# Folding the memory norm's weight into the weight splits, a second queue for the first slab, a finish by halves, and a later head scaling

## The chip, the cores and the metric

The kernel runs on one core of a Trainium2 chip. The metric is device time in microseconds from launch to the end of the program; the median of three runs of the kernel before is 1544.7 us (1544.7 to 1545.28).

## The reference

256 tokens of width 1024 go through two layers. Each layer is a mixer followed by a feed-forward part:

```
h = rms_norm(x, norm_g);  proj = h @ w_in                      # 1024 x 6672
q_a, k_a = rms_norm per head (8 heads of 64)  -> stick-breaking attention
gated linear attention, 4 heads, chunks of 64 -> o_b
mkv = rms_norm(mem, mem_norm_g) @ w_mem_kv                     # mem: 256 x 1024
m_k, m_v = split(mkv);  q_c, k_c = rms_norm per head (4 heads of 128)
o_c = softmax(q_c k_c^T) m_v
x = x + (sum_b sigmoid(gate_b) * (o_b @ w_br_b)) @ w_out
layer 0: x = x + swiglu(rms_norm(x))           # width 2816
layer 1: x = x + mixture of 8 experts, top 2   # width 3584 each
```

`rms_norm(y, g)` is `y * rsqrt(mean(y*y) + 1e-6) * g`. The factor `rsqrt(...)` belongs to a row (a token), the weight `g` to a column of `y`, which is a row of the weight matrix that follows.

## The kernel before

**Trunk.** Everything up to the experts is a list of products (`product_table`): first `mem_k` (the memory times its key weights), then `sb_q`, `sb_k`, `sb_v`, `mem_v` and so on. A product of width 512 takes its weights in four slabs of 128 x 1024 floats (512 KB). SyncE (SP) issues the slab loads in order into five buffers `w_raw`. ScalarE (ACT) rounds each slab to `w_hi` (`split`, L943), VectorE (DVE) forms the rest `w_lo = w_raw - w_hi` (`splits_until`, L1305), four slabs ahead of their use, and TensorE (PE) makes three passes (L2010 to L2012), so that a slab is 12 matmuls of 512 columns. The left operands are split in the same way: PE transposes a token tile into `ps` (`turn_tokens`, L1926), ACT takes the high part (L979), DVE the low part (L1340, `turned`).

**Order around the products.** Each engine's program is written by one function, `in_order`. After a slab, each engine calls `side()`, which runs the next step of a waiting generator, up to a `yield`; so a generator's yields decide behind which slab a step stands. `finish` runs the rest of a generator.

**The start.** SP loads memory tile 0, then `mem_norm_g` broadcast to 128 rows (512 KB), then memory tile 1, then slabs 0 and 1, then `x`, then slabs 2 on. PE passes the time with `idle_turns`. DVE multiplies each memory tile by the weight (L1354), into the buffers `tok` and `sq`, and signals `norm_done`; PE transposes these. Only the row factor `mem_rstd` is applied later, by ACT, when it takes the product out of PSUM. Then `x` is normalised: ACT squares it (L969) only after slabs 0 to 3 have been split (`splits_until(4)` in `x_norm`), DVE and GpSimd (POOL, L776) form the row factor, and DVE normalises (L1327) with `mix_norm_g`, which POOL's own DMA brings into the same `gain` buffer once the memory tiles have been weighted. The transposes of `x` into `xt1` stand behind the third slab of `mem_k` (two yields in `x_turn`), and `sb_q` needs them. POOL writes twenty small loads (`mixer_constants`, L745 to L751, for both layers) and a row of constants before it comes to the first head norm.

**The memory in layer 1.** `mem` is reloaded into `hn`; its mean squares, row factor and normalisation are made anew during the last feed-forward product.

**Head norms.** After `mem_k`, `sb_q`, `sb_k` and `ca_q`, ACT takes the result to `tok` and its squares to `sq`. DVE reduces the squares (L1513), POOL raises to the power -1/2 (L816), and DVE scales `tok` (L1526), in the first `side()` of the next product, that is behind one slab split. Three yields later PE transposes the scaled heads (L2134) and DVE writes them with their weight (L1537).

**Experts.** The experts' 1 MB slabs (`exp_raw`) stream from HBM through 22 buffers. Slots 0 to 6 are written out; later ones run in a loop whose last six slabs come one by one, each with a semaphore (`end_ready`). PE multiplies by four lanes of 32 tokens (L2140, a helper's line). At the very end, ACT copies the output block `ps` to `hs` (L1279), `scatter_last` multiplies by the selection, token tile 0 into `ps` and tile 1 into `pa`; DVE adds each whole tile to `xs` (L1895) and SP stores each tile (L708).

Of the kernel before, what the change touches and what calls it, by code (L numbers as in the profile page):

```python
# [5 lines left out]
F32 = mybir.dt.float32  # L6
# [3 lines left out]
ALU = mybir.AluOpType  # L10
# [24 lines left out]
RAW, SPLIT = 5, 5  # L35
AHEAD = SPLIT - 1
# [55 lines left out]
GAINS = 16 * LAYERS * 10  # L92
# [80 lines left out]
def trunk(nc, x_in, mem_in, mix_norm_g, w_in, sb_q_g, sb_k_g, gla_a_up, gla_a_b, gla_o_g, ca_q_g,  # L173
# [10 lines left out]
    with ExitStack() as ctx:  # L184
# [26 lines left out]
        with ExitStack() as trunk_only:  # L211
# [25 lines left out]
            cum_tri = early("cum_tri", [P, P])  # L237

# [93 lines left out]
        mem_reloaded, first_gain = sem("mem_reloaded"), sem("first_gain")  # L332
# [31 lines left out]
        y_hi, last_y = sem("y_hi"), sem("last_y")  # L364
        stored, tail_scattered = sem("stored"), sem("tail_scattered")
# [3 lines left out]
        end_ready = [sem(f"end_ready{i}") for i in range(EXP_SLABS - END)]  # L369

# [71 lines left out]
        def raw_slot(j):  # L442
            return w_raw[:, j % RAW, :]

# [113 lines left out]

        def turned_half(t, half):
            return ps[:, t * DM:(t + 1) * DM][:, half].rearrange("p (k t) -> p k t", t=P)  # L560
# [34 lines left out]
        def _(sp):  # L595
            sp.dma_start(hn[:, 0, :], memory_in[:, 0, :]).then_inc(first_tile[0], 16)
            sp.dma_start(gain[:, :], mem_norm_g[0].rearrange("(o d) -> o d", o=1)
                         .broadcast_to([P, DM])).then_inc(first_gain, 16)
            sp.dma_start(hn[:, 1, :], memory_in[:, 1, :]).then_inc(first_tile[1], 16)
# [57 lines left out]
            def expert_slabs(e, i):  # L657
# [8 lines left out]
                for j in range(end, EXP_SLABS):  # L666
                    sp.wait_ge(slab_used, i * EXP_SLABS + (PRE + j + 1 - EXP_RAW))
                    sp.dma_start(exp_slots[place(i, j)], moe_slabs[bass.ds(e, 1), j // LOAD, :, j % LOAD, :]
                                 .rearrange("e p n -> (e p) n"))\
                        .then_inc(end_ready[j - END], 16)  # L670

            first = first_slabs()
            for s, src in enumerate(flat):
                if s == 2:
                    sp.dma_start(xs[:, :, :], tokens).then_inc(x_loaded, 16)
                if s == 8 * RAW:
                    sp.dma_start(route_w[:, :, :], moe_router[0].rearrange("(k p) n -> p k n", p=P))\
                        .then_inc(route_loaded, 16)
                    with nc.allow_non_contiguous_dma(reason="1024 numbers, once"):
                        sp.dma_start(route_g[:, :],  # L680
                                     ffn_norm_g[LAYERS - 1].rearrange("(k p) -> p k", p=P))\
                            .then_inc(route_loaded, 16)
                if s >= RAW:
                    sp.wait_ge(lo_ready, s - RAW + 1)
                dst = raw_slot(s)[:, 0:sizes[s]]
                if len(src.shape) == 3:
                    dst = dst.rearrange("p (k n) -> p k n", k=src.shape[1])
                sp.dma_start(dst, src).then_inc(raw_ready[s % RAW], 16)
# [17 lines left out]
            for t in range(NT):  # L706
                sp.wait_ge(added, slots * NT + (t + 1))
                sp.dma_start(result[:, t, :], xs[:, t, :]).then_inc(stored, 16)  # L708
            sp.wait_ge(stored, NT * 16)
# [3 lines left out]
        def _(pool):  # L713
# [8 lines left out]
            gain_order = [g[l] for l in range(LAYERS) for g in (mem_norm_g, mix_norm_g, ffn_norm_g)]  # L722

            def load_gain(k):
                pool.wait_ge(norm_done, NT * k)
# [3 lines left out]
            def start():  # L729
# [6 lines left out]
                load_gain(1)  # L736
                inverse_root(mem_rstd)

            def mixer_constants():
                link(pool.memset(a_up[:, :, :], 0.0))  # L740
                for l in range(LAYERS):
                    for i, (g, n) in enumerate(((sb_q_g, SB_DH), (sb_k_g, SB_DH), (gla_o_g, GLA_DV),
                                                (ca_q_g, CA_DH), (ca_k_g, CA_DH))):
                        for r in range(0, P, n):
                            pool.dma_start(head_gains[r:r + n, l, i:i + 1],  # L745
                                           g[l].rearrange("(d o) -> d o", o=1),
                                           allow_slow_non_contiguous=True).then_inc(gains_loaded, 16)
                    for r in (0, GATE_RANK):
                        pool.dma_start(a_up[r:r + GATE_RANK, l, :], gla_a_up[l])\
# [1810 lines left out]
```

## Time and profile before

| | |
|---|---|
| median of three runs | 1544.7 us |
| profiled execution, its own time | 1545.91 us |
| its span | 1543.2 us |
| PE / DVE / ACT / POOL busy | 1499.5 / 553.9 / 430.9 / 83.5 us |
| HBM read | 477.34 MB |

The span runs from the first to the last instruction; the execution's time is 2.7 us longer. All starts are microseconds from the span's start. A PE matmul's shown duration is longer than its share of the pipeline: matmuls of one kind start closer together than they last.

### The profile page before, as it was taken

What the parts mean: (1) busy time and instruction counts of PE and PEld (TensorE: products, weight loads), DVE (VectorE), ACT (ScalarE), POOL (GpSimd) and SP (SyncE); (2) the same over time, 40 slices, a digit from 0 to 9 for tenths busy, and PEclk for the clock granted to TensorE, in tenths of its full rate; (3) what the DMA queues carried; (4) which work ended last, traced back from release to release, by engine and by line L of the source; (5) the groups of instructions that cost most, each with busy time, mean ns of one, the idle gap of its engine ahead of it and who ended that gap; (6) DMA issues with size and microseconds to landing.
All of it is one profiled execution on the core that took longest, in us unless ns stands there. A gap on an engine that the chain in (4) does not pass through costs nothing.

```text
span 1543.2 us, 27981 instructions
## 1 busy us (share of the span) xinstructions
PE 1499.5 (97%) x12518; PEld 906.8 (59%) x12518; DVE 553.9 (36%) x668; ACT 430.9 (28%) x551; POOL 83.5 (5%) x130
## 2 busy tenths in 40 slices
PE   8999999999999999999999999999999999999778
PEld 6888888788888887888335333353323533533222
DVE  5755576655567655666400101001010110010101
ACT  5556654544445557554000000000000000000000
POOL 5211100000002111001000000000000000000000
PEclk9999999999999999999999999999999999999999
DMA  8555454765655555677999999999999999999996
GB/s 274 178 152 166 149 164 153 231 189 170 205 189 184 174 149 161 207 298 306 418 403 402 416 429 429 428 428 428 428 430 429 427 428 427 430 427 427 433 426 258
DMA packets 86231, 480.20 MB, mean 311 GB/s; under 512 B 11296, under 2 KB 13408, under 8 KB 64096
## 3 DMA queue, kind: packets, MB, share of 16 engines
q1 hardware_dynamic: 84480, 474.67, 79.2%
q0 software_dynamic: 1632, 3.74, 0.8%
q8 instruction: 98, 1.61, 0.4%
q14 instruction: 21, 0.17, 0.0%
HBM read 477.34 MB, written 1.05 MB: 310 GB/s over the span
## 4 chain that ended last, share of the span: by engine, by line
PE 83%; DMA 11%; DVE 2%; POOL 2%; issue 0%; ACT 0%; SPq 0%; DVEq 0%; POOLq 0%
PE pa L2140 26%; PE ps L2140 17%; PE pa L2010 13%; PE pa L2012 12%; PE pa L2011 12%; DMA exp_raw<-in_moe_slabs 11%; DVE w_lo L1305 1%; POOL hrs L816 1%; PE ps L1926 1%; POOL head_gains L745 0%; DMA gain<-in_mem_norm_g 0%; PE ps L2313 0%; PE ps L2134 0%; PE pa L2045 0%; DVE xt L1340 0%
## 5 line engine op out<-in xcount | busy, mean ns | idle before, releaser
L2140 PE MATMUL pa<-exp_raw,xf 128*32 128x512 f32 (+1 forms) x5104 | 489.8, 540 | 20.4 <-DMA exp_raw<-in_moe_slabs 17.8
L2140 PEld LDWEIGHTS pa<-exp_raw,xf 128*32 128x32 f32 x5104 | 162.8, 110 | 327.8 <-issue 268.4
L1305 DVE TENSOR_TENSOR w_lo<-w_raw,w_hi 128x1024 fp32r<-128x1024 f32 x226 | 274.2, 1231 | 122.1 <-ACT w_hi L943 113.0
L943 ACT ACTIVATE w_hi<-w_raw 128x1024 fp32r<-128x1024 f32 (+1 forms) x228 | 236.9, 1053 | 148.7 <-PE pa L2012 147.1
L2140 PE MATMUL ps<-exp_raw,hf 128*32 128x256 f32 (+1 forms) x3040 | 245.3, 413 | 8.5 <-DMA exp_raw<-in_moe_slabs 8.2
L2010 PE MATMUL pa<-w_hi,r 128*128 128x512 f32 x600 | 240.3, 400 | 1.9 <-DVE r L1340 1.8
L2012 PE MATMUL pa<-w_hi,r 128*128 128x512 f32 x600 | 234.6, 391 | 0.0
L2011 PE MATMUL pa<-w_lo,r 128*128 128x512 f32 x600 | 234.6, 391 | 0.0
L1873 DVE TENSOR_TENSOR hs<-pa,hs 128x768 f32<-128x768 f32 (+3 forms) x32 | 23.7, 741 | 584.3 <-ACT hs L1268 584.3
L1268 ACT ACTIVATE hs<-pa 128x768 f32<-128x768 f32 (+3 forms) x32 | 20.4, 637 | 659.5 <-PE pa L2140 659.5
L2140 PEld LDWEIGHTS ps<-exp_raw,hf 128*32 128x32 f32 (+1 forms) x3040 | 116.1, 114 | 137.2 <-issue 68.8
L2010 PEld LDWEIGHTS pa<-w_hi,r 128*128 128x128 f32 x600 | 113.1, 188 | 29.4 <-issue 3.2
L2012 PEld LDWEIGHTS pa<-w_hi,r 128*128 128x128 f32 x600 | 113.0, 188 | 24.4
L2010 PE MATMUL pa<-w_hi,xt 128*128 128x512 f32 (+1 forms) x320 | 123.2, 385 | 3.0 <-DVE xt L1340 2.7
L2011 PEld LDWEIGHTS pa<-w_lo,r 128*128 128x128 f32 x600 | 113.2, 189 | 22.0
L2012 PE MATMUL pa<-w_hi,xt 128*128 128x512 f32 (+1 forms) x320 | 121.3, 379 | 0.0
L2011 PE MATMUL pa<-w_lo,xt 128*128 128x512 f32 (+1 forms) x320 | 121.3, 379 | 0.0
L2010 PEld LDWEIGHTS pa<-w_hi,xt 128*128 128x128 f32 x320 | 60.2, 188 | 16.1 <-issue 2.7
L2012 PEld LDWEIGHTS pa<-w_hi,xt 128*128 128x128 f32 x320 | 60.2, 188 | 11.3
L2011 PEld LDWEIGHTS pa<-w_lo,xt 128*128 128x128 f32 x320 | 60.3, 188 | 10.6
L1858 DVE TENSOR_TENSOR yf<-ps,yf 128x768 fp32r<-128x768 f32 (+1 forms) x7 | 5.9, 844 | 88.7 <-ACT yf L1255 88.7
L1255 ACT ACTIVATE yf<-ps 128x768 fp32r<-128x768 f32 (+1 forms) x7 | 5.0, 719 | 96.8 <-PE ps L2140 96.8
(281 smaller groups left out, 813.2 us busy)
## 6 DMA issues: line engine op xcount, KB each, us to landing
exp_raw<-in_moe_slabs SPq DMA_DIRECT2D x82, 3072.0 KB, 32.3
exp_raw<-in_moe_slabs SPq DMA_DIRECT2D x87, 1024.0 KB, 8.2
w_raw<-in_w_in SPq DMA_DIRECT2D x104, 512.0 KB, 4.4
w_raw<-in_ff_w_gate_up SPq DMA_DIRECT2D x44, 512.0 KB, 4.5
w_raw<-in_ff_w_down SPq DMA_DIRECT2D x22, 512.0 KB, 4.1
w_raw<-in_w_mem_kv SPq DMA_DIRECT2D x16, 512.0 KB, 5.1
w_raw<-in_w_out SPq DMA_DIRECT2D x16, 512.0 KB, 4.3
w_raw<-in_w_br_sb SPq DMA_DIRECT2D x8, 512.0 KB, 3.5
```

The lines of the kernel that those rows point to most:

```text
L816: pool.tensor_tensor(dst[:, 0:n], src[:, 0:n], half[:, 0:n], ALU.pow)\
L943: act.activation(dst, raw, ACT.Copy).then_inc(hi_ready, 1)
L1255: act.activation(yf[:, 0, 0:blocks * OUT], ps[:, 0:blocks * OUT], ACT.Copy)\
L1268: act.activation(hidden_rows(s, blocks), gate_up(s, 0, blocks), ACT.Silu)\
L1305: dve.tensor_tensor(dst, raw, hi.bitcast(F32), ALU.subtract)\
L1858: dve.tensor_tensor(yf[:, 1, 0:blocks * OUT], ps[:, 0:blocks * OUT], yf[:, 0, 0:blocks * OUT].bitcast(F32), ALU.subtract)\
L1873: dve.tensor_tensor(hidden_rows(s, blocks), gate_up(s, 1, blocks), hidden_rows(s, blocks), ALU.mult).then_inc(e_h, 1)
L1926: ins = pe.transpose(banks[:, t * DM + k * P:t * DM + (k + 1) * P], src[:, k * P:(k + 1) * P], ident[:, :])
L2010: pe.matmul(dst, hi, m_hi, start=first, stop=False)
L2011: pe.matmul(dst, hi, m_lo, start=False, stop=False)
L2012: return pe.matmul(dst, lo, m_hi, start=False, stop=last)
L2140: return pe.matmul(dst, a, b, start=start, stop=stop, skip_group_check=True)
```

## The change

Seven edits, in the order of the program:

1. Memory tiles go straight into `start_x` (the buffers `tok` and `sq`), unweighted, and are transposed as they are; the load of broadcast `mem_norm_g` and DVE's two multiplications go. `mem_norm_g` of both layers comes as 16 rows of 128 floats by a DMA on ACT's queue, PE turns it into 16 columns (`mem_gain`), DVE copies these. For the 16 slabs of `mem_k` and `mem_v`, the split multiplies each half slab by its column: two ACTIVATEs with a scale and two `scalar_tensor_tensor` instead of one of each.
2. Slab 0 is loaded from ACT's queue (`FIRST_ACT = 1`); SP begins with slab 1. `x` stands before slab 3. POOL loads `mix_norm_g` once slab 1 has landed.
3. In layer 0 `x` is squared after three slabs are split, not four; it is transposed behind the first slab of `mem_k`; slab 0 is multiplied tile by tile. The memory's row factor is made after that, behind the second slab, and kept for layer 1, where the memory's squares, row factor and normalisation go.
4. POOL's small loads are made per layer, ten at a time; the constants come after the first head norm.
5. DVE's head scaling stands behind the second slab split of the next product.
6. In the expert loop the last slab is loaded in two halves with a semaphore each.
7. At the end ACT copies two halves; `scatter_last` works by halves, token tile 0 into `pa` first and tile 1 into `ps`; DVE adds four half tiles and SP stores four.

Seven idle turns stand at PE's start instead of twelve, and five instead of six before the first product.

```diff
-            sp.dma_start(hn[:, 0, :], memory_in[:, 0, :]).then_inc(first_tile[0], 16)
-            sp.dma_start(gain[:, :], mem_norm_g[0].rearrange("(o d) -> o d", o=1)
-                         .broadcast_to([P, DM])).then_inc(first_gain, 16)
-            sp.dma_start(hn[:, 1, :], memory_in[:, 1, :]).then_inc(first_tile[1], 16)
+            sp.dma_start(start_x[0], memory_in[:, 0, :]).then_inc(first_tile[0], 16)
+            sp.dma_start(start_x[1], memory_in[:, 1, :]).then_inc(first_tile[1], 16)
...
+                    sp.dma_start(dst[:, 0:DM], src[:, 0:DM]).then_inc(end_ready[j - END], 16)
+                    sp.dma_start(dst[:, DM:], src[:, DM:]).then_inc(last_half_ready, 16)
...                       # GpSimd, start()
-                load_gain(1)
-                inverse_root(mem_rstd)
+                pool.wait_ge(raw_ready[1], 16)
+                load_gain(0)
...                       # ScalarE, split(s)
+                for cols, scale in gain_halves(s):
+                    if s == 0:
+                        act.wait_ge(mem_gain_ready, 1)
+                    ins = act.activation(dst[:, cols], raw[:, cols], ACT.Copy, scale=scale)
...                       # ScalarE, start()
+                act.dma_start(mem_rows[:, :], mem_norm_g.rearrange("l (k p) -> (l k) p", p=P))\
+                    .then_inc(mem_rows_loaded, 16)
+                for s in range(FIRST_ACT):
+                    act.dma_start(raw_columns(s), flat[s]).then_inc(raw_ready[s % RAW], 16)
...                       # x_turn on ACT, DVE (and PE without memory_norm)
-                yield
-                yield
+                if l > 0:
+                    yield
+                    yield
                 for t in range(NT):
                     turned(xt1, ps, t)
                 yield
+                if l == 0:
+                    memory_norm()
...                       # VectorE, x_norm
                 if l == 0:
-                    splits_until(4)
+                    splits_until(3)
                     dve.wait_ge(x_loaded, 16)
                 for t in range(NT):
                     mean_square(t)
-                dve.wait_ge(turn_ready, turns)
+                if l > 0:
+                    dve.wait_ge(turn_ready, turns)
                 for t in range(NT):
-                    normalise(xs, t)
+                    normalise(xs, t, l)
+                if l == 0:
+                    splits_until(4)
...                       # VectorE, head_work
-                dve.wait_ge(head_rs, heads)
+                heads_then = heads
+                yield
+                dve.wait_ge(head_rs, heads_then)
...                       # VectorE, the end
-            for t, bank in enumerate((ps, pa)):
+            for t, bank in enumerate((pa, ps)):
                 dve.wait_ge(tail_scattered, t + 1)
-                dve.scalar_tensor_tensor(out=xs[:, t, :], in0=bank[:, 0:DM],
...
+                for half in (LEFT, RIGHT):
+                    dve.scalar_tensor_tensor(out=xs[:, t, half], in0=bank[:, half],
...                       # TensorE, start() and the first product
-                idle_turns(12, 0)
-                for t in range(NT):
-                    turn_tokens(True, ps, t, True)
-                idle_turns(6, 0)
+                idle_turns(7, 0)
+                turn_tokens(False, ps, 0, True)
+                pe.wait_ge(mem_rows_loaded, 16)
+                pe.matmul(gain_columns, mem_rows[:, :], ident[0:LAYERS * KT, 0:LAYERS * KT],
+                          start=True, stop=True).then_inc(mem_rows_turned, 1)
+                turn_tokens(False, ps, 1, True)
+                idle_turns(5, 0)
...
+                        if p is table[0] and g == 0:
+                            for t in range(NT):
+                                pe.wait_ge(turn_lo, t + 1)
+                                ins = multiply(0, [t])
+                            ins.then_inc(slab_used, 1)
+                            side()
+                            continue
...                       # TensorE, down(), in the loop of experts
+                            if kk == 1 and j == EXP_SLABS - 1 and type(i) is not int:
+                                pe.wait_ge(last_half_ready, i * 16 + 16 * (1 - len(BLOCKS_AT)))
```

## Rows read from the trace of the kernel before

**Rows 1.** The page: PE's busy time, and PE, DMA and bandwidth in 40 slices

```profile
PE 1499.5 (97%) x12518; PEld 906.8 (59%) x12518; DVE 553.9 (36%) x668; ACT 430.9 (28%) x551; POOL 83.5 (5%) x130
...
GB/s 274 178 152 166 149 164 153 231 189 170 205 189 184 174 149 161 207 298 306 418 403 402 416 429 429 428 428 428 428 430 429 427 428 427 430 427 427 433 426 258
```

**Rows 2.** Busy time by stretch: length; PE, PEld, DVE, ACT, POOL; granted clock; DMA share, GB/s

```profile
11.60:13.60 2.00, 0.00 (x0) 0.00 (x0) 1.96 (x2) 2.00 (x3) 0.00 (x0) 1.00 1.03 396
...
27.70:29.50 1.80, 0.01 (x1) 0.00 (x0) 1.77 (x2) 1.76 (x4) 1.80 (x4) 1.00 0.84 199
30.00:33.40 3.40, 3.40 (x10) 2.62 (x9) 3.33 (x5) 1.11 (x2) 3.40 (x8) 0.50 0.79 271
...
52.70:64.50 11.80, 11.80 (x58) 9.87 (x57) 8.76 (x12) 6.07 (x8) 3.74 (x1) 1.00 0.55 181
```

**Rows 3.** Timeline of the start: start us, length us, engine, line, instruction, count, idle before

```profile
1.74 4.99 PE L1933 MATMUL pa<-ident 128*128 128x128 f32 x24 [1.74 <-POOL ident L732]
...
9.11 1.09 PE L1926 MATMUL ps<-ident,sq 128*128 128x128 f32 x8
...
12.34 1.22 DVE L1340 TENSOR_TENSOR xt<-ps,xt 128x1024 fp32r<-128x1024 f32 x1
...
13.61 0.50 PE L2010 MATMUL pa<-w_hi,xt 128*128 128x512 f32 x1 [2.07 <-DVE xt L1340]
```

**Rows 4.** DMA issues of the start: KB each, us from issue to landing

```profile
hn<-in_mem SPq DMA_DIRECT2D x1, 512.0 KB, 3.3
...
w_raw<-in_w_mem_kv SPq DMA_DIRECT2D x1, 512.0 KB, 8.3
...
gain<-in_mix_norm_g POOLq DMA_DIRECT2D x1, 512.0 KB, 7.2
...
xs<-in_x SPq DMA_DIRECT2D x1, 1024.0 KB, 10.3
```

**Rows 5.** Timeline: x's load, its squares, row factors and normalisation, then sb_q's start

```profile
3.17 0.57 SPq L675 DMA_DIRECT2D xs<-in_x  x1
...
18.46 1.05 ACT L969 ACTIVATE gates<-xs 128x1024 f32<-128x1024 f32 x1
...
20.79 1.28 DVE L1327 SCALAR_TENSOR_TENSOR hn<-xs,nrstd,gain 128x1024 f32<-128x1024 f32 x1
20.97 1.51 POOL L776 TENSOR_TENSOR nrstd<-nms,half 128x1 f32<-128x1 f32 x1 [0.40 <-DVE nms L1320]
...
29.53 0.50 PE L2010 MATMUL pa<-w_hi,r 128*128 128x512 f32 x1 [1.82 <-DVE r L1340]
```

**Rows 6.** Timeline of one head norm, and the one place where PE waits for one

```profile
47.71 3.75 POOL L816 TENSOR_TENSOR hrs<-hms,half 128x16 f32<-128x16 f32 x1 [8.09 <-DVE hms L1517]
...
51.50 1.29 DVE L1526 TENSOR_TENSOR tok<-tok,hrs 128x512 f32<-128x512 f32 x2 [2.80 <-POOL hrs L816]
...
69.68 0.93 PE L2140 MATMUL ps<-qT,kT 64*128 64x256 f32 x8 [0.22 <-DVEq L1546]
```

**Rows 7.** PE's waits in 100 to 560: for whom, us in total, times, longest

```profile
PE pa L2010 <- DVE xt L1340: 0.7, 1, 0.7
```

**Rows 8.** Timeline of the end

```profile
1523.72 0.39 ACT L1268 ACTIVATE hs<-pa 128x256 f32<-128x256 f32 x1 [16.77 <-PE pa L2140]
...
1533.51 1.94 PE L2140 MATMUL ps<-exp_raw,hf 128*64 128x512 f32 x8 [0.44 <-DMA exp_raw<-in_moe_slabs]
...
1535.50 0.60 ACT L1279 ACTIVATE hs<-ps 128x512 f32<-128x512 f32 x1 [11.39 <-PE ps L2140]
...
1537.52 1.28 DVE L1895 SCALAR_TENSOR_TENSOR xs<-ps,small,xs 128x1024 f32<-128x1024 f32 x1 [11.88 <-PE ps L2140]
1538.72 1.28 DVE L1895 SCALAR_TENSOR_TENSOR xs<-pa,small,xs 128x1024 f32<-128x1024 f32 x1
```

**Rows 9.** The two stores, and the weighting of a half tile by DVE

```profile
out<-xs SPq DMA_DIRECT2D x2, 512.0 KB, 2.7
...
L1401 DVE TENSOR_TENSOR hn<-xs,gain x4: 684/692/693, 274.7 to 282.0; 128x512 f32<-128x512 f32 x4
```

More of the change, by code:

```diff
@@ L35 @@
 RAW, SPLIT = 5, 5
+FIRST_ACT = 1
 AHEAD = SPLIT - 1
@@ L557, in trunk, with gain_halves @@
         start_x = [a[:, :, :].rearrange("p t c -> p (t c)") for a in (tok, sq)]
+        gain_columns = pa[:, 3 * BW:3 * BW + LAYERS * KT]
+        def gain_halves(s):
+            for p in table:
+                if p.name in ("mem_k", "mem_v") and p.first <= s < p.end:
+                    per = SLAB // p.width
+                    k = p.layer * KT + (s - p.first) * per
+                    return [(slice(n * p.width, (n + 1) * p.width), mem_gain[:, k + n:k + n + 1])
+                            for n in range(per)]
+            return []
         def turned_half(t, half):
@@ L705, in _ @@
                 expert_slabs(e, i)
-            for t in range(NT):
-                sp.wait_ge(added, slots * NT + (t + 1))
-                sp.dma_start(result[:, t, :], xs[:, t, :]).then_inc(stored, 16)
-            sp.wait_ge(stored, NT * 16)
+            for n in range(2 * NT):
+                t, half = n // 2, (LEFT, RIGHT)[n % 2]
+                sp.wait_ge(last_added, n + 1)
+                sp.dma_start(result[:, t, half], xs[:, t, half]).then_inc(stored, 16)
+            sp.wait_ge(stored, 2 * NT * 16)
         @block.gpsimd
@@ L720, in link @@
                 pool.wait_ge(pool_step, steps)
-            gain_order = [g[l] for l in range(LAYERS) for g in (mem_norm_g, mix_norm_g, ffn_norm_g)]
+            gain_order = [g[l] for l in range(LAYERS) for g in (mix_norm_g, ffn_norm_g)]
             def load_gain(k):
-                pool.wait_ge(norm_done, NT * k)
+                if k > 0:
+                    pool.wait_ge(norm_done, NT * k)
                 pool.dma_start(gain[:, :], gain_order[k].rearrange("(o d) -> o d", o=1)
@@ L1057, in product @@
                 l = p.layer
-                first_memory = l == 0 and p.name in ("mem_k", "mem_v")
+                of_memory = p.name in ("mem_k", "mem_v")
+                first_memory = l == 0 and of_memory
                 if first_memory:
-                    act.wait_ge(norm_rs, NT)
+                    act.wait_ge(norm_rs, NT * 2)
                 def root(t):
@@ L1278, in _ @@
             act.wait_ge(slab_used, slots * EXP_SLABS + PRE)
-            act.activation(hs[:, 0:FEW_BLOCKS * OUT], ps[:, 0:FEW_BLOCKS * OUT], ACT.Copy)\
-                .then_inc(last_y, 1)
+            for b in range(FEW_BLOCKS):
+                cols = slice(b * OUT, (b + 1) * OUT)
+                act.activation(hs[:, cols], ps[:, cols], ACT.Copy).then_inc(last_y, 1)
         @block.vector
@@ L1301, in splits_until @@
                     hi = w_hi[:, s % SPLIT, 0:w]
+                    for cols, scale in gain_halves(s):
+                        ins = dve.scalar_tensor_tensor(out=dst[:, cols], in0=raw[:, cols],
+                                                       scalar=scale, in1=hi[:, cols].bitcast(F32),
+                                                       op0=ALU.mult, op1=ALU.subtract)
+                    if gain_halves(s):
+                        ins.then_inc(lo_ready, 1)
+                        done += 1
+                        continue
                     if w < SLAB:
@@ L1349, in start @@
             def start():
-                nonlocal norms
-                for t in range(NT):
-                    dve.wait_ge(first_tile[t], 16)
-                    dve.wait_ge(first_gain, 16)
-                    dve.tensor_tensor(start_x[t], hn[:, t, :], gain[:, :], ALU.mult)\
-                        .then_inc(norm_done, 1)
+                dve.wait_ge(mem_rows_turned, 1)
+                dve.tensor_copy(mem_gain[:, :], gain_columns).then_inc(mem_gain_ready, 1)
+                dve.wait_ge(mem_gain_ready, 1)
                 turned(xt0, ps, 0)
@@ L1920, in turn_tokens @@
                     enter()
-                if normed:
+                if first:
+                    pe.wait_ge(first_tile[t], 16)
+                elif normed:
                     norms += 1
```

160 lines of the change are left out of this document (90 added, 70 removed).

## The prediction

> **What bounds the kernel now.** I read the page first, then busy time by stretch, then timelines of the stretches that the change touches. The page shows PE busy for 97% of the span, and from the middle of the span on 400 to 430 GB/s out of HBM [rows 1]. The reader is to see two regimes: a trunk in which PE never stands (the stretch 52.7 to 64.5, one product of 48 matmuls and a head norm, is 11.80 of 11.80 us busy at full clock [rows 2]; all of 100 to 560 holds one wait of 0.7 us [rows 7]), and an expert phase that runs at the bandwidth of the slabs. In both, time is won only where PE or the stream is moved as a whole. A start that is X shorter moves every later load with it, since each is released by a semaphore of the trunk's progress, so I count it in full. That leaves two stretches: the first 43 us, in which PE stood 2.07 us before its first product and 1.82 us before `sb_q` and then ran 3.4 us at half clock (0.50, that is 1.2 GHz of 2.4) [rows 2, 3, 5], and the last 10 us, a chain of single steps [rows 8].
>
> **The start.** Landings before: memory tile 0 at 0.80 + 3.3 = 4.1; slab 1 at some 2.7 + 8.3 = 11.0; `x` at 3.17 + 10.3 = 13.5 [rows 4, 5]. The broadcast of `mem_norm_g` (512 KB) goes; ahead of `x` stand the same number of bytes as before, since slab 2 moves ahead of it. At 396 GB/s [rows 2] 512 KB are 1.3 us. Slab 1 was the fifth load of that size and is now the fourth, so 9.7 or less; I take 9.0, an estimate, since tile 1 and slab 0 can now come side by side from two queues while the stream ramps up; slab 2 at 10.3, and `x` stays near 13.3.
>
> PE: seven idle turns of 4.99/12 = 0.42 us end at 4.7 [rows 3]. Tile 0 is there. Its 8 transposes take 1.1 us warm and up to 2.2 at half clock, so they end near 6.5. The turning of the gain rows is one short matmul (0.2) and a DVE copy of 16 columns (0.1), beside ACT's first 1.03 us copy. Then ACT takes the high part of tile 0 (about 1.05, as for a square [rows 5]), DVE the low part (1.22 [rows 3]), to 8.8; ACT meanwhile splits slab 0 in two halves, and DVE forms its low part in 2 x 0.66. The first product begins at about 10.1 instead of 13.61 [rows 3]. Tile by tile, slab 0 is done at 10.1 + 2.7 = 12.9.
>
> Here the gain of 3.5 us stops, because the transposes of `x` now stand behind slab 0. `x` lands at 13.3; two squares of 1.05 us [rows 5] and their reads and means end near 15.7. The `mix_norm_g` load is issued at 9.0, when slab 1 has landed, and takes 7.2 [rows 4]: 16.2. DVE normalises tile 0 from 16.1 to 17.4 and tile 1 to 18.7 (1.28 each); GpSimd's second row factor, 1.51 us beside the first normalisation [rows 5], is not later than that. PE stands from 12.9 to 17.4, 4.5 us. A stand of 1.8 us after 27.7 was followed by half clock from 30.0 to 33.4 [rows 2], one of 2.0 us before 13.6 was not (1.00 in 11.6 to 13.6 [rows 2], and the first product's matmuls start 0.23 apart); 4.5 us, I take it, will be. So tile 0's transposes take 2.1 (to 19.6), tile 1's 1.1 (to 20.7). Three slabs of 2.73 (12 matmuls at (11.80 - 0.9)/48 = 0.227 each, the 0.9 being the head's transposes [rows 2]) end `mem_k` at 28.9. `xt1` is long ready, so `sb_q` follows with no wait and, if the clock is full again by then, without the slow stretch.
>
> Before, `sb_q` began at 29.53 and paid half of 3.4 us = 1.7 for the clock, so that it was where a full-clock start at 31.2 would be. The start therefore brings 31.2 - 28.9 = 2.3 us. Bounds: PE resumes when `x` and its gain allow. Had the gain load tile 0's 3.3 us [rows 4], it would be there at 12.3, `x`'s own chain would bind, tile 1 would be normalised at 17.7, and the start would bring 3.3. If the clock stays low for a second stretch of 3.4 us it brings 2.3 - 1.7 = 0.6; if the gain also lands 2 us late, -1.4.
>
> The Trainium skill, in "DMA: Bandwidth & Descriptors", section "Rules for kernel authors", says that spreading DMAs over several issuing engines gives no bandwidth, since all run on the same 16 engines and interleave, and saves only issue time. By it the ACT queue is worth at most one issue on SP (0.4 us), and slab 0 takes half of tile 1's bandwidth. My sum has given the queue nothing. In "TensorE: Matmul & The Clock Gate", section "HAM oscillation — how this bites in real kernels", the skill has long waits of PE send it to half clock; by that rule alone the new wait behind slab 0 is what speaks against this change, and its price is the 1.1 us of slow transposes that the sum already holds, or 1.7 more in the rival below.
>
> **The rest of the trunk.** A split in two halves costs DVE 2 x 0.69 [rows 9] instead of 1.22 [rows 3], some 0.16 more, for each of 16 slabs; DVE has 3.0 of 11.8 us free [rows 2] and works four slabs ahead: 0, and 16 x 0.16 = 2.6 if that cover were gone. GpSimd writes ten small loads instead of twenty before the first head norm, and the constants after it; nothing needs these before stick-breaking, at 69.7 [rows 6]: 0. The memory norm of layer 1 goes from ACT, DVE and POOL under a PE that does not stand [rows 7]: 0. The extra 16-column matmul: 0. Head scaling: DVE stood 2.80 us for GpSimd's 3.75 us [rows 6]; one split (1.2) now fills part of it. PE's product period is 11.80 busy of 11.80 with or without, so this gives only the 0.22 us before `ps<-qT,kT`: -0.2. The other side of it: the scaling must be done before PE's transposes three slabs later; `tok` was ready at 52.7 and still is, against some 54 (29.53 + 1.7 for the clock + 11.8 + 10.9): cost 0, and one split, 1.2, for each of eight head norms if I am wrong on this order (+9.6 at most).
>
> **The end.** The last slab's first half lands about 1.2 us before the whole, at 1532.3, so PE goes on after slab 40 without its 0.44 us wait, and its second matmul pair finds the rest: it ends 0.44 earlier (1535.0) [rows 8]. ACT's first half takes 0.39 instead of 0.60, and the second runs beside the scatter, whose columns are the same in number: 0.2 more. DVE starts at 1536.9 instead of 1537.52. Four half adds at 0.66 (0.69 for a half tile [rows 9], starts a little closer, as 1.28 us adds start 1.20 apart [rows 8]) end at 1539.6 instead of 1540.0. The last store carries 256 KB instead of 512, which at some 430 GB/s [rows 1] is 0.6 less than its 2.7 us [rows 9]. Sum: 0.4 + 0.6 = 1.0. Bounds: 0.4 if a small store takes as long as a large one; 1.5 if the half adds take no longer in sum than the two whole ones, so that the 0.6 of the earlier start stays, and the store saves another 0.9 by finding the first three done; and only 0.2 if half copies, half scatters and half adds each carry 0.1 us more than the rows give, over eight such steps (1.0 - 0.8).
>
> **Sum.** -2.3 (start) - 0.2 (heads) - 1.0 (end) = -3.5. The profiled execution would go from 1545.9 to 1542.4 and its span from 1543.2 to 1539.7. The median of the runs is 1.2 us below that execution: 1544.7 - 3.5 = 1541.2.
>
> **Rivals.** (a) *Half clock holds on behind the new wait.* After 30.0 PE ran through without a pause until the clock came back; here it pauses first, until 17.4, so the clock may come back later. Slabs 1 and 2 run slow: +1.7, time 1542.9. For it: the wait of 4.5 us is the longest of the trunk. Against it: a stretch with 2 us of idle before 13.6 kept full clock. (b) *The wait is hidden anyway:* the gain lands early, `x` binds, the clock returns at once: start 3.3, end 1.5, heads 0.2, time 1539.7. For it: the gain took its 7.2 us beside a full SP queue [rows 4], which is now one load shorter. (c) *Slower:* the transposes of `x` behind slab 0 become the bound. Place: PE at the first `side()`. PE cannot go on to slabs 1 to 3, which are ready, until `x` is normalised. It breaks even with all gains elsewhere (1.2) when `mem_k` ends at 31.2 + 1.2 = 32.4, that is when tile 1's transposes end at 24.2, 3.5 us later than I have; with half clock for another stretch, 1.8 us later. A gain load of 12 us with slow clock gives 20.7 + 4.8 + 1.7 = 27.2, time 1544.7 + 3.0 = 1547.7. For it: three queues now share the 16 engines in the first 15 us. Against it: the total of bytes before that point is not larger. (d) *Head scaling late on PE:* +1.2 each, up to 1554; the rows leave over a microsecond, so it is very unlikely. (e) *The start's gain is swallowed by the slab stream*, leaving only the end: 1543.5. Against it: every slab's load waits for a semaphore that moves too.
>
> **Chances.** Forecast 0.45, (a) 0.22, (b) 0.13, (c) with (d) 0.08, (e) 0.12. What a measurement can tell from no change is about 0.2%, 3.1 us: faster means below 1541.6. The forecast lies just under that, so I split its chance 0.33 to 0.12; with (b) that is 0.46, and with 0.02 for gains that I have not priced 0.48 faster; same is 0.12 + 0.22 + 0.12 of (e), less those 0.02, 0.44; slower 0.08. Range: from (b)'s time less 0.3, 1539.4, to a little past (a) and (e), 1544.2.
>
> **What would show it.** First product near 10.1; PE idle of about 4.5 us behind slab 0; a clock of 0.50 near 16 to 20 and none near 30; `sb_q` near 28.9; span from `sb_q`'s start to the experts unchanged but for the clock; period of `sb_k` still 11.8; the last slab's wait under 0.1 us; DVE's last add ending 0.6 us closer to the end of the span than the 3.2 us (1543.2 - 1540.0) of before. I am wrong if PE's first wait for `x` ends after 19, if the clock is low twice, or if PE shows waits at the head transposes.

## The result, and the profile after

The changed kernel takes 1536.61 us (median of five runs, 1535.27 to 1537.31) against 1544.7 us before (1544.0 to 1545.28); the ratio is 0.9944, 95% interval 0.9933 to 0.9955. That is 8.1 us less, where 3.5 were forecast, and it lies below the range. The profiled execution took 1535.27 us with a span of 1533.5. It is the shortest of its five, and that of before, 1545.91 us, was above its median, so the two traces lie 10.6 us apart where the medians lie 8.1. One execution among all those reported below, of e5_slab0_on_sp, took 1880.96 us at a mean granted clock of 0.76 and is left out of its figures.

One sentence of the change's description above is wrong, and the prediction stands on it. It says that `x` is transposed behind the first slab of `mem_k`, and a comment in its diff says that the hunk on `x_turn` holds for PE too. Only ScalarE's and VectorE's `x_turn` lost their two yields; TensorE's is not in the diff and keeps them, so that TensorE transposes `x` behind the third slab, as before.

The page of the changed kernel, to be read beside [rows 1]:

```profile
PE 1494.7 (97%) x12516; PEld 905.7 (59%) x12516; DVE 552.8 (36%) x681; ACT 433.2 (28%) x564; POOL 83.4 (5%) x127
```

The busy times of the other engines are the same within 2.3 us; 4.8 of the 9.7 us by which the span fell are busy time of TensorE, with no fewer instructions to speak of, and among it are two stretches at half clock that this execution lacks, the one behind `sb_q`'s start and one of 3.4 us near 1505. TensorE's start in the timeline (start, length, engine, line, instruction, count, idle before), which answers to [rows 3, 5]:

```profile
11.04 0.47 PE L2077 MATMUL pa<-w_hi,xt 128*128 128x512 f32 x1 [1.62 <-DVE w_lo L1353]
...
19.34 1.91 PE L1989 MATMUL ps<-ident,hn 128*128 128x128 f32 x16
...
23.88 0.50 PE L2077 MATMUL pa<-w_hi,r 128*128 128x512 f32 x1
```

The first product begins at 11.04, three slabs follow, all 16 transposes of `x` come at 19.34 with no wait ahead of them, and `sb_q` at 23.88 with none either. Before, it was 29.53 behind 1.82 us of waiting. VectorE had normalised `x` between 16.22 and 18.70, while TensorE was at its third slab, slab 2. Busy time by stretch (columns as in [rows 2]):

```profile
11.10:19.30 8.20, 8.20 (x36) 6.73 (x37) 6.91 (x11) 6.08 (x10) 3.79 (x8) 1.00 1.04 391
23.90:34.90 11.00, 11.00 (x49) 9.05 (x49) 8.63 (x12) 9.57 (x14) 4.42 (x6) 1.00 0.70 211
34.90:46.70 11.80, 11.80 (x57) 9.84 (x56) 9.89 (x13) 6.08 (x8) 7.53 (x10) 1.00 0.83 276
```

TensorE does not stand from 11.04 to the attention, its clock is 1.00 in all of these stretches, and the period of a product is 11.8 us as before. The rest of the trunk only moved: the first attention matmul went from 69.68 to 62.19 (7.5 earlier), the first expert matmul from 739.7 to 732.3 (7.4). The end:

```profile
1526.43 0.66 ACT L1330 ACTIVATE hs<-ps 128x256 f32<-128x256 f32 x2 [10.26 <-PE ps L2214]
...
1529.57 1.40 DVE L1956 SCALAR_TENSOR_TENSOR xs<-ps,small,xs 128x512 f32<-128x512 f32 x2
```

Beside [rows 8]: from ScalarE's copy to the span's end it is 7.1 us instead of 7.7, and TensorE no longer waits for either of the last two slabs (before, 0.54 and 0.44 us). The first of these waits is not the change's: e3_scale_at_once, which has the changed end, shows it with 0.65 us.

### The profile page after: what moved, and what is told of

Same layout as the page of the kernel before. It is cut to its first block, busy times and chain, and to the rows that moved or that the text cites. A ratio compares the mean times of both kernels' runs of the same rounds, so it can differ in the third digit from the quotient of the medians.

```text
span 1533.5 us, 27998 instructions
## 1 busy us (share of the span) xinstructions
PE 1494.7 (97%) x12516; PEld 905.7 (59%) x12516; DVE 552.8 (36%) x681; ACT 433.2 (28%) x564; POOL 83.4 (5%) x127
## 3 DMA queue, kind: packets, MB, share of 16 engines
q8 instruction: 99, 1.62, 0.4%
## 4 chain that ended last, share of the span: by engine, by line
PE 87%; DMA 11%; DVE 1%; ACT 0%; issue 0%; DVEq 0%; ACTq 0%; SPq 0%
PE pa L2214 27%; PE ps L2214 17%; PE pa L2077 14%; PE pa L2079 13%; PE pa L2078 13%; DMA exp_raw<-in_moe_slabs 11%; PE ps L1989 1%; PE ps L2208 0%; DMA w_raw<-in_w_mem_kv 0%; PE ps L2387 0%; PE pa L2112 0%; PE ps L2364 0%; DVE hs L1933 0%; DVE w_lo L1363 0%; ACT hs L1317 0%
## 5 line engine op out<-in xcount | busy, mean ns | idle before, releaser
L1363 DVE TENSOR_TENSOR w_lo<-w_raw,w_hi 128x1024 fp32r<-128x1024 f32 x210 | 255.6, 1233 | 123.2 <-ACT w_hi L983 115.5
L983 ACT ACTIVATE w_hi<-w_raw 128x1024 fp32r<-128x1024 f32 (+1 forms) x212 | 219.9, 1053 | 128.6 <-PE pa L2079 128.1
L2078 PEld LDWEIGHTS pa<-w_lo,xt 128*128 128x128 f32 x320 | 60.3, 188 | 10.6
```

Of the source, the lines that this page charges most:

```text
L983: act.activation(dst, raw, ACT.Copy).then_inc(hi_ready, 1)
L1363: dve.tensor_tensor(dst, raw, hi.bitcast(F32), ALU.subtract)\
L2078: pe.matmul(dst, hi, m_lo, start=False, stop=False)
```

## The experiments

The theories when they began: A, the place of TensorE's transposes of `x` decides, and the order of the work on `x` on the other engines closes the wait; B, of the steps that the prediction priced near nothing (head norms, end) one or more are worth microseconds; C, the earlier first product brings all. A first set is the changed kernel once more, as base for the next three.

**after_again.** No edit.

> The changed kernel once more, on the chip of the next three, as their base. Both theories: 1536.5 us, between 1535 and 1537.5; the spread of 2 us between its runs comes from the last slabs, not from the start.

Measured 1537.25 us (1535.79 to 1538.01), ratio to before 0.9949 (0.9935 to 0.9963). So the base is 1536.6 and 1537.3 in two sets of five, and differences under 1 us between kernels are not told apart by it. The expectation put the spread between runs down to the last slabs. The trace of e2_whole_end below, which has the changed kernel's start word for word, shows a source at the start: behind a first wait of 2.48 us TensorE ran at half clock from 12.7 to 16.1, and `sb_q` began at 25.73, where it was 23.88 and 24.36 in the two traces of the changed kernel. In the expert phase every trace has slow stretches too, but there the wait for the next slab takes most of them up: in e2 48 matmuls took 7.05 us instead of 5.36, and the wait behind them fell from 1.94 us to 0.25.

**e1_turn_early.** The kernel that the prediction described.

```diff
             def x_turn(l):                  # TensorE
-                yield
-                yield
+                if l > 0:
+                    yield
+                    yield
```

> The changed kernel, and on TensorE too the transposes of x in layer 0 stand behind the first slab of mem_k, as the prediction had them. Theory A (the place of these transposes decides: TensorE works through slabs 1 and 2 while x is squared and normalised): TensorE now stands about 3.7 us behind slab 0 (from 13.8 to 17.5), mem_k ends 3.7 us later than in the changed kernel plus up to 1.1 for half clock, so time 1540.5 to 1542. Theory B (the place is indifferent, x would be there in time either way): within 0.5 us of the changed kernel.

Measured 1540.91 us (ten runs, 1539.92 to 1542.14), ratio to before 0.9974 (0.9965 to 0.9984): 3.7 over the changed kernel of its set, 4.3 over the first set. Its two slow stretches (columns as in [rows 2]) and the transposes:

```profile
12.30:15.60 3.30, 3.30 (x9) 2.16 (x7) 2.90 (x6) 3.30 (x8) 0.39 (x1) 0.50 1.04 394
...
19.10:22.40 3.30, 3.30 (x13) 2.82 (x12) 3.30 (x5) 2.58 (x4) 3.30 (x7) 0.50 0.59 166
```

```profile
17.63 2.81 PE L1989 MATMUL ps<-ident,hn 128*128 128x128 f32 x16 [1.87 <-DVE hn L1385]
```

The wait behind slab 0 ends at 17.63 (17.4 was predicted) and `sb_q` begins at 29.48 (28.9). The idle is 1.9 us and not 3.7, only because slab 0 itself ran at half clock in this execution. Theory B falls for the order, A holds: the forecast of 1541.2 was close to right for this kernel, and this kernel was not the change. That it was so close is in part luck: the first product came 1.1 us later than forecast, and half clock came twice, which the prediction had named as a sign of being wrong, though the first of these stretches, during slab 0, only took up time in which TensorE would have stood.

**e4_old_order.** TensorE as changed; ScalarE and VectorE take `x` as before.

```diff
-                    splits_until(3)         # x_norm, ScalarE and VectorE
+                    splits_until(4)
...
-                if l > 0:                   # x_turn, ScalarE and VectorE
-                    yield
-                    yield
+                yield
+                yield
```

> The changed kernel with edit 3's order on ScalarE and VectorE undone: x is squared after four slabs are split and its halves are taken behind the third split again; the loads and the folded weight stay. Theory A (the order of the work on x is what closes the 1.8 us wait before sb_q and keeps the clock up): sb_q begins 2 to 3 us later than 23.9, with a wait of 1 to 2 us before it, and the clock falls or not with it: time +2 to +4 us over the changed kernel. Theory C (the earlier first product alone brings the gain, since everything follows it): within 0.7 us of the changed kernel.

Measured 1538.06 us (1537.84 to 1540.01), ratio 0.9955 (0.9942 to 0.9969). TensorE's row before `sb_q` shows the wait back:

```profile
26.22 0.62 PE L2075 MATMUL pa<-w_hi,r 128*128 128x512 f32 x1 [1.83 <-DVE r L1397]
```

`sb_q` begins 2.3 us later than in the changed kernel, and half clock followed (0.50 from 26.5 to 29.9 in its profiled execution, 1540.01). But the medians differ by 0.8 us only, below the 2 to 4 expected, and above theory C's 0.7 by too little to tell (the two intervals allow 3 us either way). The lowest runs, in which a slow stretch is least likely, lie 2.1 to 2.6 apart (1537.84 against 1535.79 and 1535.27), and `sb_q` 1.9 to 2.3 apart in the traces. The step is shown in the trace, its price is only bounded, between nothing and some 4 us.

**e7_before_x_order.** The same step alone, on the kernel before.

```diff
-                if s == 2:                  # SP: x's load
+                if s == 3:
...
-                    splits_until(4)         # x_norm, ScalarE and VectorE
+                    splits_until(3)
...
-                yield                       # x_turn, ScalarE and VectorE
-                yield
+                if l > 0:
+                    yield
+                    yield
```

> The kernel before with only the order of x from edit 3 (x loaded behind slab 2, squared after three splits, its halves taken behind the first split on ScalarE and VectorE). Theory A: the first product still begins at 13.6, but the 1.8 us before sb_q and the slow 3.4 us behind it go: 3 to 4.5 us faster than before, near 1541. Theory C: no gain without the earlier first product, within 0.7 us of before.

Measured 1543.18 us (eleven runs, 1541.93 to 1544.31), ratio 0.9989 (0.998 to 0.9998): 1.6 less than before, between the two theories. `sb_q` begins at 28.12 and the wait before it is gone, but a new one stands in front of the attention:

```profile
68.56 0.93 PE L2146 MATMUL ps<-qT,kT 64*128 64x256 f32 x8 [1.65 <-DVEq L1552]
```

This wait was 0.22 us before [rows 6] and is 1.65 now: TensorE arrives earlier, VectorE hardly, and the attention begins only 1.1 us earlier than before. Neither theory had this; the section on the prediction says where it comes from.

**e10_before_x_order_and_heads.** e7 with edits 4 and 5: GpSimd's loads per layer and its constants after the first head norm, head scaling behind two splits.

```diff
-                dve.wait_ge(head_rs, heads)         # VectorE, head_work
+                heads_then = heads
+                yield
+                dve.wait_ge(head_rs, heads_then)
...
                 if l == 0:                          # GpSimd, x_norm
-                    mixer_constants()
-                load_gain(3 * l + 2)
+                    link(pool.memset(a_up[:, :, :], 0.0))
+                    mixer_gains(0)
+                else:
+                    load_gain(3 * l + 2)
...
+                if p is table[0]:                   # GpSimd, product
+                    mixer_constants()
+                    load_gain(2)
```

> The kernel before with the order of x (as e7_before_x_order) and with edits 4 and 5 (GpSimd's loads per layer, head scaling behind two splits); the start's loads and the weighting by VectorE stay. Theory B (the chain VectorE, GpSimd, VectorE of the head norms swallowed what e7 won at sb_q): the 1.6 us before ps<-qT,kT go, and the time is 1.5 to 3 us under e7, near 1540.8. Theory A (heads are worth 0.2): within 0.5 us of e7's 1543.2.

Measured 1539.99 us (1539.32 to 1542.16), ratio 0.997 (0.9958 to 0.9983): 3.2 under e7, and no wait before the attention. Theory B, with a little more than it had. The order of `x` alone gives 1.6 us, and with the two head norm edits 4.7. What edits 4 and 5 give alone on the kernel before was not run. What is left between this kernel and the changed one, 2.7 to 3.4 us, belongs to the earlier first product, the memory norm and the end.

**e3_scale_at_once.** The changed kernel with edit 5 undone (the diff of e10's first part, reversed).

> The changed kernel with edit 5 undone: VectorE scales the heads behind one slab split. Theory A (as predicted, hidden but for 0.2 us): within 0.5 us of the changed kernel. Theory B (with an earlier start VectorE's wait for GpSimd becomes the bound, as the 1.6 us before the first attention matmul of e7_before_x_order hints): 1 to 2 us slower than the changed kernel, seen as a wait before ps<-qT,kT.

Measured 1539.58 us (eight runs, 1537.89 to 1540.71), ratio 0.9959 (0.9944 to 0.9974): 2.3 to 3.0 over the changed kernel, more than theory B's 1 to 2; all eight runs lie above nine of the changed kernel's ten. TensorE and VectorE:

```profile
64.54 0.93 PE L2213 MATMUL ps<-qT,kT 64*128 64x256 f32 x8 [1.75 <-DVEq L1605]
```

```profile
57.61 1.29 DVE L1585 TENSOR_TENSOR tok<-tok,hrs 128x512 f32<-128x512 f32 x2 [2.14 <-POOL hrs L849]
58.82 4.06 DVE L1353 SCALAR_TENSOR_TENSOR w_lo<-w_raw,mem_gain,w_hi 128x512 fp32r<-128x512 f32 x6
```

VectorE stands 2.14 us for GpSimd, then has three splits in halves (4.06 us, where three whole ones took 3.49), then writes `kT`, and TensorE stands 1.75. In the changed kernel this wait is absent.

**e8_pool_all_first.** The changed kernel with edit 4 undone.

```diff
                     mixer_gains(0)                  # GpSimd, x_norm
+                    mixer_gains(1)
+                    mixer_constants()
                     inverse_root(mem_rstd)
...
                 if p is table[0]:               # GpSimd, product
-                    mixer_constants()
```

> The changed kernel with edit 4 undone: GpSimd issues all twenty small loads and writes the constants before the memory's row factor and the first head norm. Theory A (hidden, as predicted): within 0.5 us of the changed kernel. Theory B (GpSimd's 17 us of loads and constants stand ahead of the row factor and the first head norm, and with a start that is 7 us earlier they become the bound): the head scaling of mem_k is late, TensorE waits at its transposes, 2 to 6 us slower.

Measured 1542.85 us (eleven runs, 1541.42 to 1544.43), ratio 0.9987 (0.9978 to 0.9997): 5.6 to 6.2 over the changed kernel. Its GpSimd and TensorE rows:

```profile
30.84 1.19 POOL L804 TENSOR_TENSOR mem_rstd<-nms,half 128x1 f32<-128x1 f32 x2
...
36.34 2.49 POOL L849 TENSOR_TENSOR hrs<-hms,half 128x8 f32<-128x8 f32 x1 [4.31 <-DVE hms L1576]
```

```profile
39.70 1.94 PE L2208 MATMUL ps<-ident,tok 128*128 128x128 f32 x8 [4.60 <-DVE tok L1587]
```

The twenty loads and the constants end at 30.8, so the memory's row factor, which ScalarE needs to take `mem_k`, comes at 30.84 instead of 25.35. Everything behind it is 5 us late, TensorE waits 4.60 us at the transposes, and in this execution the granted clock is 0.50 for 6.7 us from 37.3, through the second half of that wait and for 4.3 us of work behind it. Of the edits taken back one by one, edit 4 looked like tidying and is the dearest. This is not the order of the kernel before, though: there the memory's row factor was made at 15.08, ahead of the loads, and it is edit 3 that moved it behind them. In the changed kernel VectorE has the sums for the first head norm ready at 31.2, so loads that end at 30.8 would by themselves have held up next to nothing, an estimate from these rows. So the 6 us are the price of edit 3 without edit 4.

**e2_whole_end.** The changed kernel with edits 6 and 7 undone (tile 0 still goes into `pa`).

> The changed kernel with edits 6 and 7 undone: the last slab in one load, one copy to hs, scatter, adds and stores by whole tiles (tile 0 still into pa first). Theory A (the end is worth what the prediction summed, 1.0 us): 1538.2, and the span from the last gate-up matmul to the end is 1.0 to 1.2 longer. Theory B (the end was mis-sized too, and is worth the 2.2 us by which the profiled tails differ): 1539.4.

Measured 1538.12 us (1537.32 to 1540.38), ratio 0.995 (0.9931 to 0.9969): 0.9 over one base, 1.5 over the other. Its last slab shows the old wait:

```profile
1527.90 1.94 PE L2207 MATMUL ps<-exp_raw,hf 128*64 128x512 f32 x8 [0.46 <-DMA exp_raw<-in_moe_slabs]
```

The 1.0 us of the prediction fits the medians better than the 2.2, though the intervals are as wide as the difference. The expectation on the trace missed: from the last gate-up matmul to the end it is 20.6 us here and 18.2 in the changed kernel, 2.4 more and not 1.0 to 1.2. Of this, 0.64 is the wait for the last slab but one, which edit 6 doesn't touch; the execution is also the slowest of its six, 2.3 us above their median. Where the rest comes from is open.

**e5_slab0_on_sp.** The changed kernel with slab 0 on SyncE's queue.

```diff
-FIRST_ACT = 1
+FIRST_ACT = 0
...
-                if s == FIRST_ACT + 2:
+                if s == 3:
```

> The changed kernel with slab 0 issued by SyncE behind the two memory tiles, the order of all other loads kept; only the small rows stay on ScalarE's queue. Theory A (a second queue gives no bandwidth; slab 0 only moves by an issue): slab 0 lands at the same time within 0.3 us or earlier, since it no longer shares with slabs 1 and 2 of the other queue; time within 0.5 us. Theory B (the second queue brings slab 0 earlier): first product 0.5 to 1.3 us later than 11.0, time up by as much.

Measured 1535.73 us (five runs, 1535.4 to 1535.91), ratio 0.9935 (0.9914 to 0.9956): not slower than the changed kernel, 0.9 to 1.5 us under its medians. Its issues (KB, us from issue to landing) beside those of the changed kernel:

```profile
w_raw<-in_w_mem_kv SPq DMA_DIRECT2D x1, 512.0 KB, 5.7
```

```profile
w_raw<-in_w_mem_kv ACTq DMA_DIRECT2D x1, 512.0 KB, 6.8
```

Issued at about 1.7 and landing 5.7 later, slab 0 arrives at 7.4; issued at 1.26 on the second queue it took 6.8 and arrived at 8.1, and ScalarE waited for it (it landed between 8.1 and 8.6 in all eight traces that have it on that queue). The first product begins at 10.68 instead of 11.04, but `sb_q` at 23.68 instead of 23.88, and the profiled execution (1535.81) is no shorter than the changed kernel's (1535.27): the lower median comes from runs that lie together, and 0.2 us from the start. The Trainium skill's rule that the prediction cites ("DMA: Bandwidth & Descriptors", section "Rules for kernel authors": no bandwidth from a second issuing engine) agrees with this trace. The trace goes beyond it: the load that was issued first landed later.

**e6_before_filled.** The kernel before, TensorE's wait before `sb_q` filled.

```diff
+                if p.name == "sb_q" and p.layer == 0:
+                    idle_turns(8, 2)
```

> The kernel before, with eight idle matmuls on TensorE in the wait before sb_q. Theory A (the slow 3.4 us behind that wait come from the wait and cost 1.7): clock stays at 1.00 there, sb_q still begins at 29.5, and the time is 1.7 us less, 1543.0. Theory B (the low clock doesn't depend on that wait): time within 0.3 us of before.

Measured 1545.0 us (twelve runs, 1543.66 to 1546.13), ratio 0.9998 (0.9988 to 1.0009). The clock:

```profile
14.00:17.30 3.30, 3.30 (x9) 2.60 (x8) 2.35 (x4) 2.00 (x3) 1.11 (x2) 0.50 1.03 391
27.00:33.40 6.40, 6.40 (x38) 5.57 (x37) 6.16 (x8) 4.43 (x7) 6.40 (x13) 1.00 0.86 259
```

Around the filled wait it is 1.00, where it was 0.50 in 30.0 to 33.4 [rows 2] (the eight idle turns are 16 matmuls there, and `sb_q` begins at 29.73); but the profiled execution had its slow stretch after the first wait, at 14.0, and 1.4 us of waiting before the attention. So the run does not price the clock: what is won at `sb_q` in this kernel is taken again at `kT`, as in e7 (the attention begins at 69.50, against 69.68 before), and the slow stretch may follow either of the two early waits. The price of the clock alone stays open.

**v1_first_slab_halves and v2_start.** Two tries for more. v1 passes slab 0 on by halves:

```diff
+                    if s == 0 and n_half == 0:        # ScalarE, split
+                        ins.then_inc(half_hi, 1)
...
+                        if s == 0 and n_half == 0:    # VectorE, splits_until
+                            ins.then_inc(half_lo, 1)
...
-                    pe.wait_ge(lo_ready, s + 1)       # TensorE, multiply
+                    pe.wait_ge(half_lo if s == 0 else lo_ready, s + 1)
...
+                        if s == 0 and kk == 1:
+                            pe.wait_ge(lo_ready, 1)
```

v2 adds slab 0 between the memory tiles on SyncE's queue and `idle_turns(8, 0)` for `idle_turns(5, 0)`.

> The changed kernel, and slab 0 is passed on by halves: VectorE begins its low part after ScalarE's first half, TensorE its first four-matmul rows after VectorE's. First product near 9.8 instead of 11.0, as copy and low part of a half are 0.67 and 0.7. If the start is passed on in full: 1.2 us less than the changed kernel, near 1535.7. If x binds by then (normalised by 18.7, TensorE there at 18.1): 0.6 less.

> As v1_first_slab_halves, with slab 0 issued by SyncE between the two memory tiles, and eight idle turns instead of five before the first product, so that TensorE stands less than 1 us there. Slab 0 lands 1 us earlier but ScalarE's copy of tile 0 binds (7.8): first product near 9.5; the clock stays at 1.00 through the start in every run, so the runs lie together instead of 2 us apart. Time 1534.5 to 1535.5; if the idle turns are in the way of the first product, 0.5 more.

Measured: v1 1535.83 us (1535.06 to 1536.27), ratio 0.9942 (0.9928 to 0.9956); v2 1535.56 us (1535.04 to 1536.68), ratio 0.9941 (0.9927 to 0.9955). In v1 the first product begins at 10.01, but `sb_q` only 0.2 us earlier than in the changed kernel:

```profile
23.65 0.50 PE L2085 MATMUL pa<-w_hi,r 128*128 128x512 f32 x1 [0.17 <-DVE r L1406]
```

`x` binds now: its low part is ready just too late, since its normalisation waits until 16.39 for the load of `mix_norm_g`. In v2 the first product begins at 10.18, not 9.5: its low part was ready at 9.54, but the eight idle turns ran until then, and `sb_q` begins at 23.81 behind 0.39 us of waiting for `x`. Both versions lie 0.8 to 1.7 us below the changed kernel's two medians, with runs 1.2 and 1.6 us apart instead of 2.0 and 2.2; that fits with fewer slow stretches after a shorter first wait, but was not shown; that the clock stays at 1.00 in every run of v2 was expected and can't be read from the one trace, in which it does. They are the fastest measured, with e5, and the three are not told apart.

## Why the prediction was wrong

**What bounds the kernel: half right.** In the changed kernel TensorE bounds the trunk, and its shift passes whole through the slab stream: 7.5 us at the attention, 7.4 at the first expert. Rival (e) falls. In the kernel before, TensorE was all but tied with a second chain, whose first links the rows shown before the prediction leave out:

```profile
37.96 1.67 POOL L816 TENSOR_TENSOR hrs<-hms,half 128x8 f32<-128x8 f32 x1
...
39.66 1.29 DVE L1526 TENSOR_TENSOR tok<-tok,hrs 128x512 f32<-128x512 f32 x2 [6.16 <-POOL hrs L816]
```

GpSimd is at its loads and constants from 22.5 on and comes to the first head norm at 37.96; VectorE stands 6.16 us for it. From there VectorE scales heads at 39.66, 51.50 and 63.32, some 11.83 us apart; its own work and its wait of 2.80 us for GpSimd fill each of these rounds. That is as long as TensorE's period, so the delay of the first is never made up. `kT` is ready at the end of this chain, and TensorE reaches the attention only 0.22 us before it. Moving TensorE forward alone, with this chain left as it is, could not have moved the attention. The two runs on that kernel show it. In e7 GpSimd's first load came 2.0 us earlier (21.32 instead of 23.36), one of its constants took 0.9 us longer, and the attention came 1.1 us earlier, with TensorE waiting 1.65. In e6 the chain kept its place, and so did the time. So the start's gain could be counted in full only because edits 4 and 5 move this chain, and e10 shows it moved.

**The first product: 0.9 us late.** 10.1 was predicted, 11.04 came; the difference is slab 0, for which ScalarE waited until 8.1, and the two half steps of some 0.7 us each on ScalarE and VectorE. VectorE's normalisation of `x` was put at 16.1 to 18.7 and came at 16.22 to 18.70.

**The step that failed: "the transposes of `x` now stand behind slab 0".** The diff's `x_turn` hunks were read as holding for all engines. On TensorE the two yields stayed, so slabs 1 and 2 fill the time in which `x` is prepared, and nothing waits. e1, with the edit that I had supposed, gives 1540.9 for a forecast of 1541.2, and costs 3.7 to 4.3 us of the 4.6 by which I was off. The start brought 7.3 us on TensorE's path, not 2.3: 31.2 less 23.9. It is 2.6 for the earlier first product, 1.3 for stops within `mem_k` (14.1 us from its first matmul to the wait behind it before, 12.8 from its first matmul to `sb_q` now), 1.8 for the wait and 1.7 for the clock. The last of these is read from the one traced execution; no run prices it. The Trainium skill's rule that long waits of TensorE send it to half clock ("TensorE: Matmul & The Clock Gate", section "HAM oscillation — how this bites in real kernels") was cited against the change. e1's trace agrees as far as it goes, with 0.50 behind waits of 2.54 and 1.87 us; after_again had 2.25 us of wait before its first product and 1.00 behind it, so these waits don't decide it by their length alone.

**The mis-sized term: "heads: -0.2".** Edits 4 and 5 were priced against the kernel before, in which TensorE came just late enough to hide VectorE's chain. Its 0.22 us of wait was read rightly. But the same sum moved TensorE 2.3 us forward, left the time at which it needs the heads at the old 54, and asked only whether the period stayed 11.8. Taken back from the changed kernel, edit 5 costs 2.3 to 3.0 us (e3) and edit 4 5.6 to 6.2 (e8); and e7 to e10 shows the two together giving 3.2. The total of the forecast was not off by this, since it assumed that the heads keep up, but its sharing among the terms was: "cost 0" held only as long as TensorE came late, and the start edits are what ended that. For GpSimd's loads the prediction looked for who needs the constants, and not at what stands behind them in GpSimd's queue: the first head norm in both kernels, and in the changed one the memory's row factor too.

**The end: right as far as the runs can tell.** 1.0 predicted, 0.9 to 1.5 by e2. In the traces the wait of 0.44 is gone and from ScalarE's copy on it is 0.6 less, as the sum had it; VectorE's last add ends 2.5 us before the span's end, for a forecast of 2.6.

**The memory norm of layer 1 and the 16 halved splits: 0, as predicted** from the unchanged distance between attention and experts; no run took them alone, nor edit 1 with its earlier first product, so this is read from the trace and not shown by an experiment. For the splits the cover is thin: in e3 three of them cost 0.6 us more on the chain that bound.

## What to carry to other kernels

Read an ordering edit in every engine's program, and in the one that bounds first: the same function name stands once for each engine, and a hunk that touches two of three means something else than one that touches all. When an edit moves the bounding engine forward by X, price every chain that ran beside it again with X taken off its slack, and list for each in-order queue what stands behind the work that is being moved. A bounding engine that is busy all the time can still be tied with a chain on the others: follow back who releases it at the next place where it waits at all, even for 0.2 us. Undo edits one by one from the new kernel as well as adding them to the old: here edit 4, priced at 0 from the old trace, costs 6 us to take back.

## What was not expected of the hardware

The granted clock's slow stretches at the start, each 3.4 us or twice that, did not come at the same place in every execution of nearly the same program. The kernel before had one behind the wait before `sb_q` (30.0 to 33.4) and none behind its first wait of 2.07 us; e6, e7 and e10, with the same start and 2.06 to 2.08 us of wait, had one there. The changed kernel's start ran at 1.00 behind 1.62 us of wait and behind 2.25 (after_again), and at 0.50 behind 2.48 (e2) and 2.54 (e1). The runs' mean granted clock goes with their time: of the changed kernel's first five, the two shortest have 0.999 and 0.998, the three longest 0.995 to 0.997. Runs of the changed kernel lie 2 us apart, runs of v1, with 0.56 us of idle there, 1.2. And a load issued 0.45 us earlier on a second hardware queue landed 0.7 us later than the same load behind two others on the first (8.1 against 7.4).
